# The first part of a two-block model: order, number format and buffers of its first 22 weight units and of its modulation

## The reference

```
memn = rms_norm(mem, mem_norm_g)                  # 256 x 1024
n    = rms_norm(x, mix_norm_g)
proj = n @ w_in                                   # xa 512, zu 1024, zv 1024, gate_a 1024, gate_b 1024
ya   = s5_branch(xa, ...)                         # two scans, forward and backward, 2048 complex states each
yb   = gelu(zu) * (w_s @ layer_norm(gelu(zv)) + bias)          # per head, per chunk of 128 positions
h    = x + (sigmoid(gate_a) * (ya @ w_proj_a) + sigmoid(gate_b) * (yb @ w_proj_b)) @ w_out
h    = h + attention(rms_norm(h) @ w_q, memn @ w_k, memn @ w_v) @ w_xo
h    = h + swiglu(rms_norm(h))
# second block, two layers, two streams (x and ctx)
mod  = silu(c) @ w_ada_2[l] + b_ada_2[l]          # 6 x 1024 per layer, for c and c_ctx: 48 MB of weights
```

## Time and profile before

| | |
|---|---|
| median of 3 runs | 2605.57 us (2596.77 to 2606.48) |
| profiled execution | 2614.58 us, span 2612.8 us |
| PE busy | 2291.9 us (88%) |
| DVE busy | 1711.6 us (66%) |
| ACT busy | 1034.0 us (40%) |
| POOL busy | 269.0 us (10%) |
| HBM read | 387.14 MB, 149 GB/s over the span |
| chain that ended last | PE 69%, DVE 18%, ACT 3%; PE L774 (the split products) 58% |

### The profile page before, as it was taken

The page is one execution under the profiler, slowest core; times in us unless marked ns, Lnnn a source line. Parts: engine busy times, 40 slices in busy tenths (PEclk is TensorE's granted clock), DMA queues, the critical chain, the costliest instruction groups (busy, mean ns, idle before and its releaser), DMA issues.

```text
span 2612.8 us, 42890 instructions
## 1 busy us (share of the span) xinstructions
PE 2291.9 (88%) x17529; PEld 2115.4 (81%) x17529; DVE 1711.6 (66%) x2085; ACT 1034.0 (40%) x1196; POOL 269.0 (10%) x277
## 2 busy tenths in 40 slices
PE   4766678988999988989999968989998986998998
PEld 4731177987999987889999957889998985888998
DVE  5689942456555897756548877756546887775554
ACT  4301142344434445534334426534334434544332
POOL 2857400001000001000000011000000002100000
PEclk8977797999999999999999979999999997999999
DMA  5358752442655543344556512245555542333552
GB/s 159 113 210 323 264 170 81 158 133 82 199 193 179 162 146 97 114 161 155 183 177 186 162 65 81 97 146 161 193 177 155 160 129 65 97 97 115 192 186 87
DMA packets 289715, 392.52 MB, mean 150 GB/s; under 512 B 7911, under 2 KB 256030, under 8 KB 282911
## 3 DMA queue, kind: packets, MB, share of 16 engines
q1 hardware_dynamic: 285868, 383.59, 45.0%
q10 hardware_dynamic: 3282, 5.74, 0.7%
q0 software_dynamic: 416, 1.08, 0.3%
HBM read 387.14 MB, written 3.15 MB: 149 GB/s over the span
## 4 chain that ended last, share of the span: by engine, by line
PE 69%; DVE 18%; ACT 3%; issue 3%; POOL 1%; DVEq 0%; ACTq 0%
PE L L774 58%; PE M L774 4%; DVE w_rest L375 3%; PE M L912 1%; DVE m L2023 1%; DVE gate L2023 1%; DVE work L2218 1%; DVE m L1729 1%; DVE n_rest L1738 1%; PE M L1160 1%; POOL work_r L752 1%; DVE work L2323 1%; DVE s5z L2018 1%; DVE work L2195 1%; DVE rstd L1726 1%
## 5 line engine op out<-in xcount | busy, mean ns | idle before, releaser
L774 PE MATMUL L<-n_high,w_high 128*128 128x256 f32 x3584 | 1031.0, 288 | 52.9 <-DVE n_rest L1738 18.1
L774 PE MATMUL L<-n_rest,w_high 128*128 128x256 f32 x3584 | 1013.6, 283 | 0.0
L774 PE MATMUL L<-n_high,w_rest 128*128 128x256 f32 x3584 | 1013.2, 283 | 0.0
L375 DVE TENSOR_TENSOR w_rest<-raw,w_high 128x2048 fp32r<-128x2048 f32 x311 | 714.2, 2298 | 290.3 <-PE L L774 285.3
L369 ACT ACTIVATE w_high<-raw 128x2048 fp32r<-128x2048 f32 x311 | 594.8, 1914 | 430.5 <-PE L L774 392.8
L774 PEld LDWEIGHTS L<-n_high,w_high 128*128 128x128 f32 x3584 | 691.2, 193 | 83.8 <-issue 54.8
L774 PEld LDWEIGHTS L<-n_high,w_rest 128*128 128x128 f32 x3584 | 692.3, 193 | 0.0
L774 PEld LDWEIGHTS L<-n_rest,w_high 128*128 128x128 f32 x3584 | 691.0, 193 | 0.4
L774 PE MATMUL L<-hid_high,w_high 128*128 (+1 forms) x704 | 196.6, 279 | 6.1 <-DVE hid_rest L2120 6.1
L774 PE MATMUL L<-hid_high,w_rest 128*128 (+1 forms) x704 | 195.6, 278 | 0.0
L774 PE MATMUL L<-hid_rest,w_high 128*128 (+1 forms) x704 | 195.5, 278 | 0.0
(11 more groups left out here) (369 smaller groups left out, 2981.6 us busy)
## 6 DMA issues: line engine op xcount, KB each, us to landing
raw<-in_w_in SPq DMA_DIRECT2D x116, 1024.0 KB, 5.5
raw<-in_w_ffn SPq DMA_DIRECT2D x99, 1024.0 KB, 5.2
raw<-in_w_ada SPq DMA_DIRECT2D x48, 1024.0 KB, 8.0
raw<-in_w_out SPq DMA_DIRECT2D x16, 1024.0 KB, 5.0
raw<-in_w_gate SPq DMA_DIRECT2D x11, 1024.0 KB, 5.3
raw<-in_w_up SPq DMA_DIRECT2D x11, 1024.0 KB, 5.2
raw<-in_w_down SPq DMA_DIRECT2D x11, 1024.0 KB, 4.9
raw<-in_w_four SPq DMA_DIRECT2D x6, 1024.0 KB, 5.1
```

The source lines that it names most:

```text
L375: nc.vector.tensor_tensor(w_rest[:, u.first % 2, :], raw[:, u.first % 4, :], w_high[:, u.first % 4, :].bitcast(F32), ALU.subtract).then_in ...
L774: ins = mm(dst, a, b, start=first and i == 0, stop=last and i == 2, skip_group_check=skip)
```

## The change

`schedule()` loses mem_k, mem_v, xa, zv, zu and gate_a; it begins with glu. These 22 units and the 48 of the modulation form one list, EARLY, whose order is written out, and all are read from `raw` in plain float32. x is loaded, transposed and normed first, into `n_x`; mem second, into `n_mem`. ScalarE copies the transposed tokens out of M and squares them. VectorE makes the powers and the first table, and norms mem; GpSimd makes b_bar, the block matrices and tables 1 to 7. The tables (`s5h`) lie over `w_high`, `n_x` and `n_mem` over `n_high` and `n_rest`. The out product goes over the four column groups inside and over the four terms outside, into one bank. After the scan `n_x` is split into `n_high` and `n_rest` for gate_b, and the modulation is transposed back after proj_a.

```diff
+def early_order():
+    fill = [(name, k) for name in ("zu", "mem_k", "mem_v", "zv") for k in range(4)]
+    start = [("xa", 0), ("xa", 1)] + [("ada", a) for a in range(8)]
+    scan = [[fill[2 * b]] + [("ada", 8 + 4 * b + a) for a in range(4)] + [fill[2 * b + 1]] for b in range(8)]
+    end = [[("ada", 40 + 2 * k), ("ada", 41 + 2 * k), ("gate_a", k)] for k in range(4)]
+    return start, scan, end
...
 # SP: order of the first loads
+            sp.dma_start(ident[:, :], consts["ident"]).then_inc(ident_in, 16)
+            sp.dma_start(x_rows, t["x"][0].rearrange("(a p) n -> p a n", p=P)).then_inc(x_in, 16)
             sp.dma_start(gate[...], t["mem"][0]...).then_inc(mem_in, 16)
+            def load_early(i):
+                name, k = EARLY[i]
+                slot = early_slot(i)
+                if i >= 4:
+                    sp.wait_ge(early_done, i - 3)
...
+            load_early(0)
+            load_early(1)
 (the parameters, masks)
+            load_early(2)
+            load_early(3)
 (lambda rows, dft64, swap, pair_ones)
+            for i in range(4, len(EARLY)):
+                load_early(i)
...
 # TensorE
+            def early_cols(x, acts, chunk=None):
+                w, bank = early_begin(x)
+                if chunk is None:
+                    for o in range(2):
+                        for c in range(DC):
+                            ins = mm(bank[:, o * T:(o + 1) * T], w[:, c, o * P:(o + 1) * P], acts[:, c, :], start=c == 0, stop=c == DC - 1)
...
-                for r in range(4):
-                    for k, (i, z) in enumerate(zip((0, 0, 1, 1), zset[b % 2])):
-                        ins = mm(L[32 * r:32 * r + 32, 2 + b % 2, 0:T], CT[:, i, 4 * d + c, 32 * r:32 * r + 32], z[:, r, :],
+                for k, (i, z) in enumerate(zip((0, 0, 1, 1), zset[b % 2])):
+                    for r in range(4):
+                        ins = mm(L[32 * r:32 * r + 32, 3, 0:T], CT[:, i, 4 * d + c, 32 * r:32 * r + 32], z[:, r, :],
...
+            turn_tokens(x_rows, tokens_turned)
+            pe.wait_ge(params_in, 16 * (len(COLS) + 1 + 4 + 2 * LAYERS))
 (transposes of the parameters)
+            token_sums(0, 2)
+            pe.wait_ge(mem_in, 16)
+            turn_tokens(rows2, tokens_turned)
+            token_sums(1, 3)
+            pe.wait_ge(s5_coef_rows, 1)
+            pe.wait_ge(ms_ready, 1)
 (coefficients back)
+            early_cols(("xa", 0), n_x, lambda c: pe.wait_ge(scaled, SCALED[0] + c + 1))
+            early_cols(("xa", 1), n_x)
+            for a in range(8):
+                modulation(a)
+            pe.wait_ge(s5_blk, 10)
 (transposes of the blocks)
             s5_in_product(0)
-            half = 0
-            for b, upto in enumerate((2, 3, 5, 7, 8, 10, 12, 12)):
+            for b in range(8):
+                if b:
+                    s5_out_product(b - 1)
+                early(EARLY_SCAN[b][0])
                 if b < 7:
                     s5_in_product(b + 1)
-                while half < upto:
-                    modulation(half)
-                    half += 1
-                s5_out_product(b)
+                for x in EARLY_SCAN[b][1:]:
+                    early(x)
+            s5_out_product(7)
+            for k in range(4):
+                for x in EARLY_END[k]:
+                    early(x)
 (SGU transposes after k == 0; then the SGU products, glu, proj_a, the modulation's transposes, gate_b)
...
 # VectorE, after its rows of coefficients
+            token_norm(0, hx, lambda c: col("mix_norm_g", c), 2, n_x)
 (coefficients copied; powers: for each of two tables four doublings of six operations, and squarings of five)
+            dve.wait_ge(early_out, 2)
             V.tensor_copy(xaR, xaT[:, :, ::-1]).then_inc(xa_ready, 1)
+            link(V.tensor_tensor(c4, up(hc_), low(lc_), ALU.mult))
+            link(V.tensor_tensor(s4, up(hs_), low(ls_), ALU.mult))
+            link(V.tensor_tensor(c4, c4, s4, ALU.subtract))
+            link(V.tensor_tensor(s4, up(hs_), low(lc_), ALU.mult))
+            link(V.tensor_tensor(part, up(hc_), low(ls_), ALU.mult))
+            link(V.tensor_tensor(s4, s4, part, ALU.add))
+            lam_dots()
+            token_norm(1, memT, lambda c: col("mem_norm_g", c), 3, n_mem)
```

More of the change, by code:

```diff
@@ L72, in schedule @@
 def schedule():
-    s = [("mem_k", 4), ("mem_v", 4), ("xa", 2), ("ADA", 0),
-         ("zv", 4), ("zu", 4), ("gate_a", 4), ("glu", 1), ("proj_a", 2), ("gate_b", 4), ("proj_b", 4),
+    s = [("glu", 1), ("proj_a", 2), ("gate_b", 4), ("proj_b", 4),
          ("out", 4), ("mem_q", 4), ("mem_o", 4), ("ffn_up", 22), ("ffn_down", 11)]
@@ L126, with early_slot @@
 UNITS = _number_units()
-BEFORE_ADA = FIRST["zv"]
-ADA_UNITS = LAYERS * 3 * DC
+def early_order():
[4 more added lines that the diff above has]
+    return start, scan, end
+EARLY_START, EARLY_SCAN, EARLY_END = early_order()
+EARLY = EARLY_START + [x for part in EARLY_SCAN + EARLY_END for x in part]
+EARLY_AT = {x: i for i, x in enumerate(EARLY)}
+DENSE_AT = {x: i for i, x in enumerate([x for x in EARLY if x[0] != "ada"])}
+def early_slot(i):
+    return (i + 4 - len(EARLY) % 4) % 4
+EARLY_LANDED = [sum(early_slot(i) == slot for i in range(len(EARLY))) for slot in range(4)]
 class Unit:
@@ L159, in build @@
         raw = sb("raw", [P, RAW, UNIT])
+        over = ExitStack()
+        with over:
+            s5h = over.enter_context(nc.sbuf_tensor("s5h", [P, 8192], F32))
         w_high = sb("w_high", [P, RAW, UNIT], F32R)
@@ L609, in load_ffn @@
                 load_rows(name + "down", down_w)
[L611 to L626, removed]
-                sp.dma_start(raw[:, v % 4, :], t["w_ada_2"][l, k * P:(k + 1) * P, g * UNIT:(g + 1) * UNIT]).then_inc(landed[v % 4], 16)
-            load_cols("zv", w_in, HALF + D)
-            load_cols("zu", w_in, HALF)
-            load_cols("gate_a", w_in, HALF + 2 * D)
             load(Unit(FIRST["glu"]), t["s5_w_glu"][0].rearrange("(k p) n -> p k n", p=P),
@@ L741, in make_table @@
                 pool.sem_inc(s5_tab, 1)
-            for b in range(8):
+            for b in range(1, 8):
                 make_table(b)
@@ L1010, in _ @@
-            pe.wait_ge(s5_coef_rows, 1)
-            pe.wait_ge(ms_ready, 1)
-            coefficients_back()
-            cols_linear("mem_k", chunk=normed_chunk(0))
-            rows_linear("mem_v", before={1: lambda: turn_blocks(0), 3: lambda: turn_blocks(4)})
-            pe.wait_ge(turned_out, 4 + 8)
-            turn_tokens(1, rows2)
-            norm(1, 10)
-            cols_linear("xa", chunk=normed_chunk(1))
-            def modulation(half):
-                grp = half // 2
-                if half == 0:
-                    pe.wait_ge(silu_ready, 1)
-                    pe.wait_ge(bank_free[0], after("xa", 0))
-                    pe.wait_ge(bank_free[1], after("xa", 1))
-                if half % 2 == 0 and grp >= 2:
-                    pe.wait_ge(ada_row, grp - 1)
-                for a in range(4 * half, 4 * half + 4):
-                    v, kc = BEFORE_ADA + a, a % 8
-                    pe.wait_ge(landed[v % 4], 16 * (v // 4 + 1))
-                    for q in range(4):
-                        ins = mm(L[32 * q:32 * q + 2, grp % 2, :], silu_c[:, kc, :], raw[:, v % 4, q * 512:(q + 1) * 512],
-                                 start=kc == 0, stop=kc == 7, skip_group_check=True)
-                    ins.then_inc(ada_done, 1)
@@ L1038, in s5_in_product, with early @@
+            def early(x):
+                name, k = x
+                if name == "ada":
+                    modulation(k)
+                elif name in ("zv", "mem_v"):
+                    early_rows(x, n_x if name == "zv" else n_mem)
+                else:
+                    if x == ("mem_k", 0):
+                        pe.wait_ge(scaled, SCALED[1] + DC)
+                    early_cols(x, n_mem if name == "mem_k" else n_x)
             def s5_in_product(b):
                 d, c = (1 if b < 4 else 0), b % 4
-                pe.wait_ge(xa_ready, 1)
@@ new lines, in _ @@
+            dve.wait_ge(sgu_mm, 1)
+            for b in range(4):
+                x = zu[:, 2 * b:2 * b + 2, :].rearrange("p a t -> p (a t)")
+                V.tensor_tensor(x, x, M[:, b, :], ALU.mult).then_inc(sgu_out, 1)
+            dve.wait_ge(n_again_high, 1)
+            dve.wait_ge(early_done, len(EARLY))
+            V.tensor_tensor(n_rest[:, :, :], n_x[:, :, :], n_high[:, :, :].bitcast(F32), ALU.subtract).then_inc(n_again, 1)
+            linear("glu")
+            evacuated(dve, "glu")
```

619 lines of the change are left out of this document (348 added, 271 removed).

## The result

The changed kernel takes 2529.22 us at the median (2526.12 to 2534.04), the one before 2603.47 (2596.77 to 2606.48) beside it: ratio 0.972 [0.9694, 0.9746], 74 us less. The forecast was 2494, its own range 2478 to 2515, the wide one 2464 to 2545. The sign was right and the time is inside the wide range, but outside the forecast's own. It lies near the price of the second rival (2532). The trace shows that rival's mechanism in most tiles, but at well under half its price; the rest of the difference has other causes, so that the two numbers meet is chance.

What follows compares the result with a forecast made beforehand. Bound: the chain of waits to gate_b at 471.6 us, VectorE's scan within it. Preparation, scan and what follows were priced to 360, 112 us less: 2494 from median 2605.6; own range 2478 to 2515 (0.55), eight in ten 2464 to 2545.

Steps and rivals of the forecast that it cites:

- rival 2: Scan: ring and clock set the tile; clock falls in each pause, out product 3.6; scan 38 us longer, 2532; chance 0.18.
- the end part: Behind the scan on TensorE: eight modulation units 7.6, four of gate_a 27.8, eight transposes 0.9 us, ending at 314.7.
- Tile 0 starts at 86: End of preparation: VectorE's first scan tile starts at 86 us, bounds 76 to 110, against 147.9 before.
- I take 20: Preparation: parameters land at 20 us, bounds 18 to 27, with x, mem and two weight units ahead on SP's queue.
- the powers: Preparation on VectorE: 89 linked operations, 23 us, or 35 if GpSimd's bbar work beside them slows them.
- most of the powers are too small for that: Preparation: argument that GpSimd would not slow most of VectorE's power operations as it slows adds (2.84 against 1.22 us).
- rival 1: Preparation stays long: parameters at 27, powers and table slowed by GpSimd, tile 0 at 110; 24 us later, 2518; chance 0.12.
- a sign that it was wrong: Preparation: the first table and the powers taking over 45 us together would show the prediction wrong.
- 24.6, just above VectorE's 23.2: Scan tile on TensorE: 20.9 us work, 3 waiting for the ring, 0.7 lost clock; TensorE sets the pace.
- Rival 3: Half clock all along: tile 41.8 us, end 70.8 instead of 35.4, gate_b near 543; 2677 us; chance 0.03.
- Rival 5: Head start not taken: one early wait holds tile 0 until 147; gain only behind the scan, 50 us; 2556; chance 0.02.
- Rival 4: Everything overlaps better: tile 0 at 78, VectorE's 23.2 as pace, SGU warm; 24 us less, 2470; chance 0.10.

Runs made afterwards that it cites:

- Parameters first: Changed kernel with the first two weight units issued behind the parameters on SP's queue, not ahead of them; 2522.25 us, ratio 0.9694.
- Waits filled: Changed kernel with eight extra 128x256 products per scan tile where TensorE waits for the ring, result unchanged; 2517.44 us, ratio 0.9669.
- modulation spread: Changed kernel with each scan tile ordered plain unit, two modulation units, plain unit, two modulation units; 2503.34 us, ratio 0.9605.
- both edits: Changed kernel with two modulation units per tile moved behind the second plain unit and the parameters issued before the first weight units; 2491.95 us, ratio 0.9556.

## Why the prediction was right in its sign and 35 us off

**What held.** Preparation, the scan and what lies behind it each gave time, and nothing after gate_b did. The plain unit (7.1 for a forecast 6.95), a modulation unit (0.92 for 0.9), the out product (1.9 for 2.0), the end part (36.5 for 36.3: 305.6 to 342.1), the hidden layer norm, the SGU products (19.2 for 18) and the wait at gate_b's second unit (1.4 for 2) came about as priced. The sums took 5.67, not the cold 6.5.

**First mis-sized term: preparation.** "Tile 0 starts at 86": it started at 95.7. "I take 20" for the parameters' landing was the first error: 26.96, at the upper bound of 27. The price was taken from bytes and from a median of landings, with the small issues overlapping; the trace shows that they do not overlap but stand behind the two units on the queue, 7.56 us for the first one. Parameters first, which takes the two units out of their way, brought 20.27 and tile 0 7.2 us sooner. The sums were quicker than forecast and the coefficients followed closely, so VectorE had them at 41.5 for 37. The second was the powers, 30.9 instead of 23: for ten microseconds beside GpSimd's work on bbar most of the small operations took 0.6 to 1.15 us instead of 0.2, which is some 6 of the 8 us. "most of the powers are too small for that", the argument against rival 1, was wrong; the smallest ones suffered most. The table took 15.2, not 13. The norm of memory gave some back (7.4 with the lambda sums, for 10; its eight scalings took 3.26, with no GpSimd beside them). Powers and table took 46 us together, just above the 45 that the prediction had named as a sign that it was wrong.

**Second mis-sized term: the tile.** "24.6, just above VectorE's 23.2": it was 26.7, and 27.2 in the tile shown. Against the forecast that tile has 0.6 more of pause (3.64 instead of 3), 0.9 on the fourth modulation unit and 1.9 on the second plain unit, less the 0.7 allowed for the clock. On average over the seven tiles it is 1.0 more of pause (4.0 for 3), 0.1 on the fourth modulation unit and some 1.9 on the second plain unit, less the 0.7. So the pauses were mis-sized by 1.0 us; the larger part of what was missing is their effect on what follows, taken at 0.7 and near 2 in the runs. That is rival 2 without its terms for the out product, 2.1 us a tile instead of 5.2. Waits filled shows the clock's part, and modulation spread shows that both the waits and the clock go when the load has time to land. The forecast gave this rival 0.18 and leaned on the bursts of 7 us between the pauses; the earlier trace rows had already shown the clock at 0.50 behind such a pause. "HAM oscillation — how this bites in real kernels" in the Trainium skill's "TensorE: Matmul & The Clock Gate" is nearer to the trace than the forecast: behind the waits the second plain unit starts on the slow clock in six of eight tiles (8.91 against 7.17), though not in the two others, and the first unit of the next tile does not (7.17).

**The sum.** The last out product was to end at 278.4 and ended at 305.6, 27.2 later: 9.7 from tile 0's start, 14.7 from seven tiles at 2.1, and 2.8 more between tile 0 and tile 1, where the second plain unit waited 2.4 us for its load (109.43). glu to proj_a took 1.4 more than forecast, the SGU 1.2. Together gate_b came 30 us later than forecast (388.1 for 358). In the profiled executions the saving was 88.5 for 112: 83.5 ahead of gate_b, 5 in the rest, which is less than that part varies by. By the medians it was 74, 14 less than between the two profiles; the forecast had taken the whole saving from the median, and where these 14 us lie no trace shows. The median of before was 2603.5 in the comparison, 2 us below the one forecast from. That 2529 is inside the wide range is partly luck: the range was made wide for rivals 1 and 2, and a part of each came true.

**What the rivals were worth.** Rival 3 (half clock throughout) fell: 0.91. Rival 5 fell: tile 0 started at 95.7. Rival 1 was half true (tile 0 at 95.7, between 86 and 110). Rival 2 was right in kind and cost 15 us in the scan, not 38. Rival 4 was false for this kernel; with both edits, where VectorE sets the pace, the time came to 2492.

## What to carry to other kernels

In a ring of buffers, count for each load the time from the slot's release to its use, and place the short units so that a long one stands in every such interval; average bandwidth says nothing of it. A pause costs its length and, behind most of them here, then the clock of what follows it (some 1.8 us on a plain unit). Put small transfers that something waits for ahead of large ones on the same queue: at the start of this kernel the queue held their issue as well.

## What the runs showed of the hardware that was not expected

- A small transfer's issue took 7.56 us (6.60 in a second profile) directly behind two units of 1 MB on one queue, with x and mem, 2 MB more, just ahead of them, and 0.42 us without the units. Behind four units later in the start, the issue of another small one took 0.46.
- Beside GpSimd, VectorE's products of 32 columns took up to 1.15 us instead of 0.21, a factor of 5, where those of 1024 columns went from 1.23 to 2.95. Holding GpSimd back moved the slowing to the next work (3.26 to 6.81 for eight scalings).
- TensorE without an idle moment from 306 us on fell to the lower clock at 346.9, 4.8 us into the SGU products (0.41 to 0.72 a pair), while plain units with no gaps held 1.00. What it is in the SGU products that does this was not tried.
- Sixteen products, four accumulating into each of four column groups, took 1.9 us when the groups alternate and 4.5 us group by group.
